# Two transformer models on one core: order of the first products, weight splits and modulation loads at the latent hand-overs

## The reference, cut to what matters

```python
def swiglu(u, wi, wo):
    g, up = jnp.split(u @ wi, 2, axis=-1)
    return (jax.nn.silu(g) * up) @ wo

def hybrid_layer(h, hc, c, c_ctx, w_ada, b_ada, g, w_in, ...):
    m = (jax.nn.silu(c) @ w_ada + b_ada).reshape(c.shape[0], 1, N_MOD, D_MODEL)
    mc = (jax.nn.silu(c_ctx) @ w_ada + b_ada).reshape(1, 1, N_MOD, D_MODEL)
    pre = rms_norm(t, g[gi]) * (1 + mm[i + 1]) + mm[i]            # ahead of a sub-block
    post = t + wres * mm[i + 2] * rms_norm(y, g[gi])              # behind it
    h, hc = post(h, swiglu(pre(h))), post(hc, swiglu(pre(hc)))    # ffn a
    u, uc = pre(h), pre(hc)
    o = latent_mix(u @ w_in, ..., context_mix(uc @ w_in))         # in, attention
    h, hc = post(h, o @ w_o), post(hc, oc @ w_o)                  # attn_out
    h, hc = post(h, swiglu(pre(h))), post(hc, swiglu(pre(hc)))    # ffn b
```

## Time and profile before

| | |
|---|---|
| median of 3 runs | 3029.91 us |
| the profiled execution | 3031.82 us, span of its instructions 3030.0 us |
| TensorE busy | 94% of the span, mean granted clock 0.954 |
| VectorE, ScalarE, GpSimd busy | 59%, 38%, 6% |
| chain that ended last | PE 86%, DVE 6%, ACT 3%, issue 2%, DMA 2% |
| memory traffic | 539.74 MB, mean 178 GB/s |

### The profile page before, as it was taken

The page is one execution under the profiler, slowest core; times in us unless marked ns, Lnnn a source line. Parts: engine busy times, 40 slices in busy tenths (PEclk is TensorE's granted clock), DMA queues, the critical chain, the costliest instruction groups (busy, mean ns, idle before and its releaser), DMA issues.

```text
span 3030.0 us, 39714 instructions
## 1 busy us (share of the span) xinstructions
PE 2856.5 (94%) x16596; PEld 2379.8 (79%) x16596; DVE 1795.6 (59%) x2675; ACT 1158.1 (38%) x1552; POOL 191.8 (6%) x172
## 2 busy tenths in 40 slices
PE   6999999998899999999989888999989999897898
PEld 5887678786776877888878577888878888886898
DVE  3555368666534886747642666647567376546554
ACT  3333357534433763222422642222422224335433
POOL 0000000000000000000220330000210001202000
PEclk7999999998899998999989988999989999899899
DMA  7657789745477973434321012434324354221352
GB/s 293 247 195 292 288 306 370 286 145 231 185 282 274 367 292 141 170 120 190 137 91 70 15 56 112 174 116 188 134 93 179 111 195 146 91 98 57 118 192 81
DMA packets 77907, 539.74 MB, mean 178 GB/s; under 512 B 8752, under 2 KB 9008, under 8 KB 18720
## 3 DMA queue, kind: packets, MB, share of 16 engines
q1 hardware_dynamic: 76016, 529.87, 46.6%
q0 software_dynamic: 1712, 7.33, 0.9%
HBM read 536.12 MB, written 1.05 MB: 177 GB/s over the span
## 4 chain that ended last, share of the span: by engine, by line
PE 86%; DVE 6%; ACT 3%; issue 2%; DMA 2%; POOL 1%; SPq 0%; DVEq 0%; ACTq 0%
PE bank L1055 10%; PE bank L1311 9%; PE bank L1312 9%; PE bank L1313 9%; PE bank L1346 4%; PE bank L1348 4%; PE bank L1347 4%; PE bank L1246 4%; PE bank L1247 4%; PE bank L1248 4%; PE bank L1466 2%; PE bank L1271 2%; PE bank L1273 2%; PE bank L1238 2%; PE bank L1272 2%
## 5 line engine op out<-in xcount | busy, mean ns | idle before, releaser
L2141 DVE TENSOR_TENSOR w_lo<-raw,w_hi 128x2048 fp32r<-128x2048 f32 (+1 forms) x356 | 772.9, 2173 | 299.4 <-ACT w_hi L1663 298.7
L1663 ACT ACTIVATE w_hi<-raw 128x2048 fp32r<-128x2048 f32 (+1 forms) x356 | 645.6, 1816 | 523.8 <-PE bank L1348 240.6
L1311 PE MATMUL bank<-h_hi,w_hi 128*128 128x512 f32 (+1 forms) x1472 | 535.5, 364 | 42.7 <-DVE w_lo L2141 21.2
L1312 PE MATMUL bank<-h_lo,w_hi 128*128 128x512 f32 (+1 forms) x1472 | 532.1, 361 | 0.0
L1313 PE MATMUL bank<-h_hi,w_lo 128*128 128x512 f32 (+1 forms) x1472 | 531.9, 361 | 0.0
L1311 PEld LDWEIGHTS bank<-h_hi,w_hi 128*128 128x128 f32 x1472 | 287.6, 195 | 85.6 <-DVE w_lo L2141 22.5
L1312 PEld LDWEIGHTS bank<-h_lo,w_hi 128*128 128x128 f32 x1472 | 288.0, 196 | 39.4
L1313 PEld LDWEIGHTS bank<-h_hi,w_lo 128*128 128x128 f32 x1472 | 287.4, 195 | 39.8
L2193 DVE CUSTOM_DVE_ANT_0 bank<-raw,raw 128x1024 f32<-128x1024 f32 x240 | 286.4, 1255 | 0.0
L1901 ACT ACTIVATE quads<-bank 128x512 f32<-128x512 f32 (+1 forms) x88 | 47.9, 544 | 586.5 <-PE bank L1313 586.5
L1346 PE MATMUL bank<-act_hi,w_hi 128*128 128x512 f32 (+1 forms) x770 | 270.0, 351 | 0.9 <-DVE w_lo L2141 0.9
(11 more groups left out here) (469 smaller groups left out, 4533.0 us busy)
## 6 DMA issues: line engine op xcount, KB each, us to landing
raw<-in_w_experts SPq DMA_DIRECT2D x192, 1024.0 KB, 6.1
raw<-in_w_ffn_in SPq DMA_DIRECT2D x88, 1024.0 KB, 4.8
raw<-in_w_mods SPq DMA_DIRECT2D x60, 1024.0 KB, 7.2
raw<-in_w_wide SPq DMA_DIRECT2D x60, 1024.0 KB, 6.9
raw<-in_w_ffn_out SPq DMA_DIRECT2D x64, 704.0 KB, 4.2
raw<-in_w_c_in SPq DMA_DIRECT2D x20, 1024.0 KB, 4.8
raw<-in_w_a_in SPq DMA_DIRECT2D x12, 1024.0 KB, 6.3
raw<-in_w_b_in SPq DMA_DIRECT2D x12, 1024.0 KB, 5.5
```

Of the source, the lines that this page charges most:

```text
L1311: pe.matmul(o, hi[:, f, :], h_hi[:, k, cols], start=(k == 0), stop=False)
L1312: pe.matmul(o, hi[:, f, :], h_lo[:, k, cols], start=False, stop=False)
L1663: act.activation(w_hi[pair_of(k)][:, 0:size], raw_of(k)[:, 0:size], ACT.Copy).then_inc(sem("hi_ready"), 1)
L2141: dve.tensor_tensor(w_lo[pair_of(k)][:, 0:size], raw_of(k)[:, 0:size], w_hi[pair_of(k)][:, 0:size].bitcast(F32), ALU.subtract).then_inc(*r ...
```

## The change: what it does

Three edits. First, `first_two` takes its order from a table. Stream 0 of two is as before. Stream 1 has chunk 0 k 0 and 1, chunk 1 k 0 and 1, then chunk 0 k 2 to 7, then chunk 1 k 2 to 7. A lone stream has chunk 0 k 0 to 3, chunk 1 k 0 and 1, chunk 0 k 4 to 7, chunk 1 k 2 to 7. Second, the split of chunk 2 moves to step 0, ahead of the evacuation or of silu and gating; in the FFNs the split of chunk 3 moves into step 1, behind `upper` and `lower` of chunk 0 and ahead of `wide` of that step. Third, the load of a `w_wide` chunk moves one weight chunk later in SP's order; in `ffn0b` and `ffn1a` the first one comes behind chunk 2 and the next two behind chunk 3. The ring of slots is dealt out in the order of loads, so slots change hands accordingly.

```diff
+        def wide_behind(name, at):
+            early = name in ("ffn0b", "ffn1a")
+            steps = {2: (0,), 3: (1, 2)}.get(at, (at - 1,) if at > 3 else ()) if early else (at - 1,)
+            return [i for s in steps if (i := wide_after(name, s)) is not None]
...
                         out.append((name, at))
-                        if (i := wide_after(name, at)) is not None:
-                            out.append(("ada", i))
+                        out += [("ada", i) for i in wide_behind(name, at)]
...
-        LAG = 3
+        of = lambda c, *ks: [(c, k) for k in range(*ks)]
+        FIRST_TWO = {2: of(0, KT) + of(1, KT), 1: of(0, 2) + of(1, 2) + of(0, 2, KT) + of(1, 2, KT)}
+        FIRST_ALONE = of(0, 4) + of(1, 2) + of(0, 4, KT) + of(1, 2, KT)
...
-                    if (i := wide_after(name, at)) is not None:
+                    for i in wide_behind(name, at):
                         load(("ada", i), A["w_wide"][i - WIDE_AT])
...
+                order = FIRST_TWO if len(ss) == 2 else {1: FIRST_ALONE}
                 for x in ss:
-                    lag = 0 if x else KT if len(ss) == 2 else LAG
-                    for k in range(KT + lag):
-                        if k < KT:
+                    for at, (c, k) in enumerate(order[len(ss) - x]):
+                        if c == 0 or x:
                             pe.wait_ge(*W("h_ready", (k // 2, x), at=norm))
-                            marks(0, x, k, product(0, x, k))
-                        if x == 0 and k == lag:
-                            sem_, key, at = y_key(before, KT - 1, (ss[-1],))
-                            pe.wait_ge(*W(sem_, key, at=at))
+                        elif k == 0:
+                            sem_, key, at_ = y_key(before, KT - 1, (ss[-1],))
+                            pe.wait_ge(*W(sem_, key, at=at_))
                             pe.wait_ge(*raw_done((name, 1)))
-                        if k >= lag:
-                            marks(1, x, k - lag, product(1, x, k - lag))
+                        marks(c, x, k, product(c, x, k))
...
 # ScalarE, linear (VectorE the same with split_lo)
                     if c == 0 and name in NEXT.values():
+                        split_hi((name, 2))
+                    elif c == 1 and name in NEXT.values():
                         pass
...
 # ScalarE, ffn (VectorE the same with split_lo; its wide(name, at) stays last in the step)
                     if at == 0 and name in NEXT.values():
+                        split_hi((name, 2))
+                    elif at in (1, 2) and name in NEXT.values():
                         pass
                     elif at + 1 < 2 * FFN_CH:
                         split_hi((name, at + 1), size=SLOT if (at + 1) % FFN_CH < FFN_UP else DOWN)
...
                         if c:
                             upper(tag, c - 1)
+                        if at == 1 and name in NEXT.values():
+                            split_hi((name, 3))
```

More of the change, by code:

```diff
@@ L959, in first_two @@
                 for x in ss:
-                    lag = 0 if x else KT if len(ss) == 2 else LAG
-                    for k in range(KT + lag):
-                        if k < KT:
+                    for at, (c, k) in enumerate(order[len(ss) - x]):
+                        if c == 0 or x:
                             pe.wait_ge(*W("h_ready", (k // 2, x), at=norm))
-                            marks(0, x, k, product(0, x, k))
-                        if x == 0 and k == lag:
-                            sem_, key, at = y_key(before, KT - 1, (ss[-1],))
-                            pe.wait_ge(*W(sem_, key, at=at))
+                        elif k == 0:
+                            sem_, key, at_ = y_key(before, KT - 1, (ss[-1],))
+                            pe.wait_ge(*W(sem_, key, at=at_))
                             pe.wait_ge(*raw_done((name, 1)))
-                        if k >= lag:
-                            marks(1, x, k - lag, product(1, x, k - lag))
-                        if x == 0 and len(ss) == 2 and k in later:
-                            later[k]()
+                        marks(c, x, k, product(c, x, k))
+                        if x == 0 and len(ss) == 2 and at in later:
+                            later[at]()
             def first_pair(name):
@@ L2464, in linear @@
                     if c == 0 and name in NEXT.values():
+                        split_lo((name, 2))
+                    elif c == 1 and name in NEXT.values():
                         pass
@@ L2683, in ffn @@
                             lower(tag, c - 1)
+                        if at == 1 and name in NEXT.values():
+                            split_lo((name, 3))
                         wide(name, at)
```

## The result

The changed kernel takes 2988.94 us (median of 4 runs, 2983.29 to 2990.58) where the kernel before takes 3027.39 in the same comparison: ratio 0.9866, 95% interval 0.9843 to 0.9890, that is 41 us less, between 33 and 48 (the medians themselves differ by 38.5). Compared again, it has 2990.59 against 3032.81, ratio 0.9857 (0.9839 to 0.9875). The prediction was 2994, 35.8 us less (ratio 0.9882): direction and stops as forecast, the size some 5 us too small. This first interval still holds 0.9882, the second one just leaves it out. The profiled execution has a span of 2988.2 us and a mean granted clock of 0.964 (before 0.954).

A forecast was written before the change was run, and what follows sets the result against it. TensorE, busy for 94% of the span, was taken as the bound. Waits of 24.8 us and 11 of clock, 35.8 off 3031.8, gave 2996.0; with the median 1.9 lower, 2994, range 2987 to 3010 for 8 in 10.

The forecast's parts named there:

- Parts 1 to 4: Ahead of the third chunk at five hand-overs: reordered products and earlier splits save 24.8 us of TensorE waits.
- Part 3: `ffn0b` and `ffn1a`: 14.7 us less waiting for both; DVE's reordered work leaves the fifth chunk 0.1 us to spare.
- Rival (b): Two FFN joins: DVE late by one wide chunk each, 10 us return, 15 with lower clock: 3009; chance 11%.
- Rival (d): Early product order: slices come late, ACT is not released early, half the wait gains go: about 3008; chance 3%.
- Rival (c): FFNs: wide rows land after DVE wants them; 232 us slower than before if one landing late; chance 3%.
- Part 5: Wide loads moved behind the next weight chunk: cost zero, no gain, fifteen microseconds to spare.
- Part 6: Behind the five stops: the lower clock goes with them, 11 us less, bounds 0 and 11.
- rival (a): At the five hand-overs: stops go but the clock falls all the same, 24.8 us alone, 3005; chance 12%.

The follow-up runs named there:

- a1: The changed kernel with the old order of first products, moved splits and new loads kept; 3015.18 us, ratio 0.9946 to the kernel before.
- a2: The changed kernel with the splits of the third and fourth chunk back in their old places; 3005.21 us, ratio 0.9916 to the kernel before.
- a3: The changed kernel with the loads of the wide rows back in the old order; 3002.16 us, ratio 0.9908 to the kernel before.
- the filled one: The kernel before with extra matmuls, results overwritten, in the five stops ahead of the third chunk; 3010.40 us, ratio 0.9927 to the kernel before.
- changed_again: The changed kernel, unaltered, compared and profiled again beside the kernel before; 2990.59 us against 3032.81, ratio 0.9857.
- g: The changed kernel with the split of `ffn1b`'s first chunk moved from `attn_out1`'s last step into the join; 2990.51 us, ratio 0.9848 to the kernel before.

## Why the prediction was right in its mechanism and wrong in one size

Parts 1 to 4, the stops: right to 4%. 24.8 us were predicted, 23.9 measured. `in0` 4.3 predicted and 4.14 measured, the two FFNs 7.35 and 7.21 each, `in1` 4.5 and 4.14, `ffn1b` 1.3 and 1.21. In the three FFNs the trace names gating as what ended the last stop, as forecast. In `in0` and `in1` it names none; the split ends 0.1 us ahead of both restarts (1550.05 + 2.29 = 1552.34 in `in0`). The old order (a1) and the old splits (a2) put back show that both were needed.

The table load that moved behind the upper half took 1.28 us and was followed at once by silu, as the earlier trace rows had it; with the drain that the Trainium skill gives ("ScalarE: Activation LUTs", section "What ACT_TABLE_LOAD costs") the stops of the FFNs would have been about 1.9 us, an estimate from that page's figure, instead of 0.77. The trace disagrees with the page here:

```profile
1833.53 1.28 ACT L1912 ACT_TABLE_LOAD   x1
1834.82 0.60 ACT L1912 ACTIVATE quads<-bank 128x512 f32<-128x512 f32 x1
```

Part 3's account of DVE was a few tenths of a microsecond too good: the fifth chunk has nothing to spare instead of 0.1 us, and loses 0.1 to 0.2. Rival (b), late by a whole wide row, did not come. The prediction's reading of the earlier trace rows had one wait too many, the 0.44 us inside `ffn1b`, which its sum did not use. Rival (d)'s 3008 should have been 3006 by its own terms (2994 + 24.8/2); it did not come either. Rival (c) did not come either: no wait on a wide row appears. Part 5 was right that the late loads cost nothing and wrong that they gain nothing: the slot that they leave to the fourth chunk, which part 3 names without a price, is what keeps 5.3 us of stops and lower clock out of `ffn0b` and of `ffn1a` each (a3).

Part 6 is the step that failed. It took 11 us, and 11 us as the upper bound too: the time lost behind the five restarts, from the length of the low spells there. That much was right. The clock is at 1.00 behind all five, with stops of 0.20 to 0.77 us ahead of them, in all three profiles, and rival (a) is out. But the changed part regained 15.0 us beside the stops, not 11. The sum put the spells at the lower clock inside the hand-overs at no change, without a reason, and they did change: together those of `ffn1a`, `in1` and `ffn1b` had 68 us in each profile of before and 44 to 51 in those of the changed kernel. These three stretches are 4.5 us shorter than predicted. In `ffn1a` and `in1` this comes with the change; in `ffn1b` the spell is shorter in every other version too, the filled one included (27.3 us in before, 14 to 24 elsewhere). The cause of either is open. What lies between 38.9 us and the 42 of the medians in the second comparison (between 38 and 49) is in no profile and within what the runs scatter.

## What to carry to other kernels

When a stop on a weight split ends last, ask what stands ahead of the split on each of its two engines, and how early the buffer's last reader can be made to end: reordering products bought 3.6 us a time for no instruction. A ring of slots is an order too: an early split of a chunk is lost again (5.3 us at each of two hand-overs here) if its load waits for the slot of something consumed later, so loads should stand in the order in which they are consumed. A TensorE stop of 4 us cost another 2.5 behind it through the clock in this kernel; count it, and don't take nearby spells at the lower clock as fixed.

## What the runs showed of the hardware that was not expected

A stop can be made harmless for the clock without being shortened: 28 matmuls of 512 columns in a stop of 8 us left the granted clock at 1.00. Ten of them, 2.5 us, in a wait of about 4 us kept it at 1.00 from there to the end of the hand-overs to `ffn0b` and `ffn1a`, where 20.5 us had been at 0.50 in changed_again. Stops of up to 1.10 us ahead of the third chunk left the clock at 1.00 in every profile; one of 1.72 us did not (before, `ffn1b`), and of the three of about 2.6 us in a3 one did not either. Whether a hand-over's low spell ends early goes in steps, not smoothly: the stretch of `in1` was 379.04, 379.05 (g), 379.06 or 384.33 us, never between.
